# Three output projections: first additions ahead of other VectorE work, last weights rounded first

## What is computed

```
def hybrid_layer(x, ...):
    h = rms_norm(x, norm_g)
    proj = h @ w_in
    ...
    y = jnp.concatenate([ya, yb, yc, yd], axis=-1) * jax.nn.silu(gate)
    return x + y @ w_out
```

## Time and profile before

| | |
|---|---|
| median of 3 runs | 2443.67 us (2440.84 to 2444.39) |
| the profiled execution | 2440.04 us, of it span 2438.3 us |
| TensorE busy | 2292.2 us, 94% |
| VectorE, ScalarE, GpSimd busy | 1144.0 us (47%), 897.2 us (37%), 902.2 us (37%) |
| mean granted clock of TensorE | 0.977 |
| chain that ended last | TensorE 78%, VectorE 11%, issue 5%, ScalarE 3%, GpSimd 2% |

### The profile page before, as it was taken

One profiled execution on the slowest core, in us unless ns is written; L12 is line 12 of the kernel. 1 busy time (PEld: TensorE's weight loads), 2 busy tenths in 40 slices (PEclk: granted clock), 3 DMA queues, 4 the chain that ended last, 5 costly groups with the idle time before them and its releaser, 6 DMA issues.

```text
span 2438.3 us, 35106 instructions
## 1 busy us (share of the span) xinstructions
PE 2292.2 (94%) x14164; PEld 1750.0 (72%) x14164; DVE 1144.0 (47%) x2230; ACT 897.2 (37%) x1492; POOL 902.2 (37%) x962
## 2 busy tenths in 40 slices
PE   7899999999999999879998999999999999998898
PEld 7777878986695876545696778789857859664456
DVE  4267244515346127766333762346162542277662
ACT  4433224714334334333433332164143344333341
POOL 2265212224525411555423542222345172115552
PEclk9989999999999999989998999999999999999899
DMA  4110232230100113100321003413201002030003
GB/s 152 39 36 2 87 113 83 82 126 1 36 18 1 50 57 121 61 1 1 139 70 56 19 1 104 143 36 120 88 1 36 18 3 93 12 147 35 1 1 130
DMA packets 92018, 141.30 MB, mean 58 GB/s; under 512 B 18352, under 2 KB 65488, under 8 KB 91856
## 3 DMA queue, kind: packets, MB, share of 16 engines
q1 hardware_dynamic: 91856, 139.05, 16.6%
HBM read 105.48 MB, written 33.55 MB: 57 GB/s over the span
## 4 chain that ended last, share of the span: by engine, by line
PE 78%; DVE 11%; issue 5%; ACT 3%; POOL 2%; DMA 0%; SPq 0%; POOLq 0%; DVEq 0%; ACTq 0%
PE psum L248 36%; PE psum L517 12%; PE psum L1430 6%; PE psum L1392 3%; PE psum L1413 3%; PE psum L1378 3%; PE psum L1416 3%; PE psum L1418 3%; PE psum L767 2%; POOL w_lo L202 2%; DVE gla_A L790 2%; PE psum L1437 1%; PE psum L1035 1%; PE psum L1816 1%; DVE mla_nm L1551 1%
## 5 line engine op out<-in xcount | busy, mean ns | idle before, releaser
L202 POOL TENSOR_TENSOR w_lo<-w_raw,w_hi 128x512 fp32r<-128x512 f32 (+3 forms) x240 | 321.8, 1371 | 846.9 <-ACT w_hi L189 846.9
L248 PE MATMUL psum<-h_hi,w_hi 128*128 128x512 f32 x768 | 207.5, 411 | 0.0
L1625 POOL TENSOR_TENSOR mla_acc<-mla_acc,mla_p 128x512 f32<-128x512 f32 (+3 forms) x160 | 159.8, 1014 | 105.5 <-ACT mla_p L1484 105.5
L248 PE MATMUL psum<-h_lo,w_hi 128*128 128x512 f32 x768 | 195.7, 394 | 0.0
L248 PE MATMUL psum<-h_hi,w_lo 128*128 128x512 f32 x768 | 195.1, 394 | 0.0
L248 PE MATMUL psum<-w_hi,h_hi 128*128 128x256 f32 (+3 forms) x1280 | 183.7, 286 | 0.0
L248 PE MATMUL psum<-w_hi,h_lo 128*128 128x256 f32 (+3 forms) x1280 | 180.2, 284 | 0.0
L248 PE MATMUL psum<-w_lo,h_hi 128*128 128x256 f32 (+3 forms) x1280 | 179.4, 283 | 0.0
L189 ACT ACTIVATE w_hi<-w_raw 128x2048 fp32r<-128x2048 f32 (+3 forms) x60 | 113.6, 1894 | 177.6 <-PE psum L517 168.5
L1625 POOL TENSOR_TENSOR fox_acc<-fox_acc,fox_p 128x512 f32<-128x512 f32 (+3 forms) x160 | 150.0, 958 | 75.5 <-ACT fox_p L1484 75.4
L248 PEld LDWEIGHTS psum<-h_hi,w_hi 128*128 128x128 f32 x768 | 146.1, 196 | 33.5 <-issue 3.1
(11 more groups left out here) (325 smaller groups left out, 4423.9 us busy)
## 6 DMA issues: line engine op xcount, KB each, us to landing
w_raw<-in_w_in_dram SPq DMA_DIRECT2D x38, 1024.0 KB, 5.4
out_dram<-x_rows SPq DMA_DIRECT2D x64, 512.0 KB, 2.7
x_rows<-out_dram SPq DMA_DIRECT2D x56, 512.0 KB, 5.3
w_raw<-in_w_out_dram SPq DMA_DIRECT2D x16, 1024.0 KB, 6.3
x_first<-in_x_dram SPq DMA_DIRECT2D x8, 512.0 KB, 7.0
x_rows<-in_x_dram SPq DMA_DIRECT2D x8, 512.0 KB, 5.1
w_raw<-in_w_in_dram SPq DMA_DIRECT2D x2, 1088.0 KB, 8.5
w_raw<-in_w_in_dram SPq DMA_DIRECT2D x2, 1056.0 KB, 5.2
```

The costliest lines, as they stand in the source:

```text
L202: last = pool.tensor_tensor(self.w_lo[c["set"]][:, at], self.w_raw[c["set"]][:, at], self.w_hi[c["set"]][:, at].bitcast(F32), ALU.subtract)
L248: last = pe.matmul(o, lhs, rhs, start=(kk == 0 and n == 0), stop=(kk == KT - 1 and n == 2))
L1625: pool.tensor_tensor(acc, acc, p, ALU.add).then_inc(self.acc_done.sem, 1)
```

## The change

Three first additions move forward in VectorE's order: `outA.add(0, 0)` ahead of `conv(1)`, `outB.add(0, 0)` ahead of `rotate_queries`, `outC.add(0, 0)` ahead of the rest of the second half, `outC.rest(1)`. On ScalarE, the rounding of the weights `outC1` moves ahead of the wait for the attention's last output and of `outC.round(1)`. No instruction is added or removed; GpSimd's, TensorE's and SyncE's orders are the same.

```diff
 def scalar_last_out(act, k, a):
     a.attC.end_act(act)
+    k.round_chunk(act, a.layer, "outC1")
     a.attC.wait_y(act)
     a.outC.round(act, 1)
-    k.round_chunk(act, a.layer, "outC1")
...
 def vector_last_out(dve, a):
     a.attC.end_dve(dve)
+    a.outC.add(dve, 0, 0)
     a.outC.rest(dve, 1)
-    a.outC.add(dve, 0, 0)
     a.outC.add(dve, 0, 1)
...
     lru.scales_dve(dve, link)
+    a.outA.add(dve, 0, 0)
     lru.conv(dve, link, 1)
-    for h, n in OUT_GROUPS:
+    for h, n in OUT_GROUPS[1:]:
         a.outA.add(dve, h, n)
...
     mla0.gain_queries(dve, link)
+    a.outB.add(dve, 0, 0)
     mla0.rotate_queries(dve, link)
-    a.outB.add(dve, 0, 0)
     mla1.mean_dve(dve, link, 0)
```

## The result

| | before | after |
|---|---|---|
| median of 4 runs each | 2442.86 us (2440.84 to 2444.39) | 2414.16 us (2411.39 to 2418.40) |
| ratio | | 0.9883, 95% interval 0.9869 to 0.9897 |
| the profiled execution | 2440.04 us | 2418.40 us, of it span 2416.6 |
| mean granted clock of TensorE | 0.977 | 0.977 |

The change makes the kernel faster by 28.7 us, interval 25 to 32. Between the two profiled executions the difference is 21.6 us (2440.04 - 2418.40), the forecast of the sum (2418.3) to 0.1 us. What failed is thus not the order of events, but two sizes: what the waits cost in the median run, above all those of B, and the time of the kernel before from which the gain was taken. The rest of this text is about that.

The account below looks back on a forecast made before the run. TensorE, busy 94%, was taken as the bound, waiting for VectorE's additions and low weights. A 3.9 + 2.6, B 3.1 + 3.1, C 4.7 + 4.7 = 22.1 us, less 2 x 0.2 = 21.7; 2443.67 - 21.7 = 2422.0 us, range 2415 to 2430.

Parts of the forecast that it names:

- the sum: Losses of projections A, B and C over both layers: 22.1 us, less 2 x 0.2, gives 21.7 us.
- B: Projection B, addition ahead of the rotation: TensorE's wait and slower first part go, 3.1 us in each layer.
- the six waits: TensorE waiting for VectorE's first addition in three projections of two layers, 15.6 us in all; all gone, chance 71%.
- A: Projection A, addition ahead of conv(1): all loss goes, 3.9 us in layer 0 and 2.6 in layer 1.
- `conv(1)` behind the additions: Projection A: conv(1) ends at 339.7 instead of 335.64, its reader over 33.6 us on; cost 0.
- The rotation's cover: Projection B: rotated queries are read 25 us on, ten times the delay, so moving the rotation costs 0, bound 2.4 us.
- C: Projection C: the bank wait and the low-weights wait go, loss 4.7 us per layer before a small remaining wait.
- The remaining wait of 0.2 us for the low weights: Projection C: TensorE still waits 0.2 us per layer for low parts, bounds 0 and 0.9 us.
- The fourth addition and the rest behind it: Projection C: the addition waits for row 3, delaying rest(1) to about 1194.4; cover 6.3 us, cost 0.
- Rivals: Low weights late 2426, 9%; clock against 2428, 8%; clock in favour 4%; stall returns 2428, 4%; nothing won 2%; slower 2%.
- as many fewer 2416: Later stages: two or three fewer low-clock stretches, each up to 2.5 us, give 2416 us; chance 4%.

Follow-up runs that it names:

- the filled kernel: Kernel before plus 12 extra matmuls into an unread bank inside projection B's wait, no addition moved: 2437.22 us against 2440.78, ratio 0.9986.
- the repeated profile: The changed kernel run and traced once more, against the kernel before: 2413.87 us (5 runs), ratio 0.9894, profiled execution 2412.33 us.
- the filled stages: Projection B to C in the kernel before with extra matmuls in B's wait, and with them in A and C too: 2437.22 and 2435.51 us.

## Why the prediction was wrong: the order was right, two sizes were short

- **What bounds the kernel; the six waits.** Right. All six and both of the waits for low weights are gone, and nothing came in their place.
- **A.** Right: forecast 6.5 us, measured 6.6 by stages (8.1 in time, interval 5 to 11), with the luck that the clock's share in one trace was near its mean. `conv(1)` behind the additions costs nothing, as said.
- **B.** Here the sum is short. "With a slower first part the loss is 3.1" per layer prices the wait by one execution in which the clock did not fall behind it. Measured are 4.5 us per layer by stages (3.0 to 6.0), and in time 10.0 and 11.7 us for both layers, where 6.2 was forecast. Two terms were missing: the seam, 0.16, and 1.2 us of clock in the mean. That the wait has such a cost beyond its length is shown by the filled kernel, which wins 3.4 us (1.2 to 5.6) with the wait left in place. The rotation's cover was right: in the attention's opening the wait for the rotated second half, `mla_q` L1673, is 16.1 us with and without the move.
- **C.** Right in order and size: forecast 9.4, measured 9.3 in time, 10.2 by stages. The remaining wait of 0.2 us for the low weights was 0.07 (1.16 us for 1.09 at 1185.07). The Trainium skill (GPSIMD Engine Reference, Specifications) was the better guide here: by its rule the low parts would be quicker without the rest of y beside them. The runs agree, and give the price: 5.07 us alone, 5.29 with an overlap in part, 7.00 and 7.08 beside it. The prediction named the rule and took 5.29. What it did not see is that the two edits of C need each other for that reason: the additions alone would have made the kernel slower by 6.9 us.
- **The fourth addition and the rest behind it.** Right: row 3 landed 3.5 us after its issue (forecast 3.4 to 5.4), and group (1,0) waits for nothing.
- **The seam.** The sum measured each loss to the shown end of the last matmul, but a group without a wait starts 0.16 us before it. Six times that is 0.96 us, a plain omission: the text ahead of the prediction says that groups start about 0.15 us before the end of the group ahead.
- **From the sum to the time.** Two steps together left the range: the gain of 21.7, which had the waits of B at 3.1 per layer, and the base of 2443.67. "2443.67 - 21.7" mixed a median of three runs, 2 to 4 us above the kernel's medians of 11 to 21 runs, with a gain read from one execution. The text saw a profiled run at the low end of the runs and 1.6 us of clock in it that might not recur, and drew only on the loss: it never asked what clock the other waits cost in executions in which this one had been lucky. By stages over all traces the gain is 6.6 + 9.0 + 10.2 = 25.8 us; with 2440.5 for the kernel before (the mean of its medians 2439.67, 2441.58, 2440.0 and 2440.78) that gives 2414.7, and 2414.16 and 2413.87 were measured. Of the 7.8 us between 2422.0 and 2414.16 the base has 3.2 and the gain 4.1, and either alone would have left the forecast in its range (2440.5 - 21.7 = 2418.8, 2443.67 - 25.8 = 2417.9).
- **The agreement of the two profiled executions to 0.1 us is partly chance.** The one after is the longest of its kernel's four runs; its stage from C to the next A is 349.2 us, where the repeated profile has 346.3.
- **Rivals.** None of those named happened. The one nearest is the clock, "as many fewer 2416", given 4%: right in its sign, but argued from chance in later stages, where at least part of the cause is that each wait removed also takes away the low clock that may follow it: behind A's wait 7 of 16 times and never in 8 stages with the move, behind B's 5 of 12 and never in 8. The Trainium skill (TensorE: Matmul & The Clock Gate, What's actually happening) says that the number of slow matmuls at a kernel's start varies from run to run of one kernel. Of a pause in the middle it does not say so; the runs show it there, and a cost that comes in some executions has a mean that belongs in the sum.

What stays open: why the attention has less time at 1.2 GHz in the filled stages (20.5 us) than in the moved (24.3) and the untouched ones (26.4), and whether that, from 4, 8 and 12 stages, is more than scatter. If it is only scatter, 0.7 us of B's 1.2 us of clock per layer are shown, and the other 0.5 are not.

## What to carry to other kernels

Here a wait of the bounding engine, TensorE, cost its length and the mean of the low clock behind it; read the second from several executions, or at least don't set it to zero because one profile shows none. Start from a base of many runs when the gain is read from one execution and the range is a fraction of a per cent. And when one edit shifts two engines' work against each other, price the overlap: two edits that gain 9 us together lost 7 when only one of them was made.

## What the runs showed of the hardware

- GpSimd's four 128x512 subtractions and VectorE's 128x2048 subtraction from SBUF slow each other: 5.07 and 2.28 us apart, 7.00 to 7.08 and 3.05 to 3.13 together, all of GpSimd's loss in one of its four (3.3 us for 1.3).
- Extra matmuls in a wait made the kernel faster: 3.4 us (1.2 to 5.6) for 24 of them, 12 in each of two waits of 3.0 us.
- Behind the same wait of 3.0 us the granted clock fell to 1.2 GHz in 5 of 12 stages and not in the other 7, behind A's wait of 2.3 to 2.5 us in 7 of 16. Executions of one and the same kernel on one chip differ by 8 to 12 us, 0.3 to 0.5%.
